# Gate and up products of both FFNs: six of eight couples of k-tiles as seven block products, one weight sum made by an accumulating transfer

## The reference

```python
def swiglu_ffn(x, w_gate_up, w_down):
    gate, up = jnp.split(x @ w_gate_up, 2, axis=-1)
    return (jax.nn.silu(gate) * up) @ w_down
...
        h = h + swiglu_ffn(rms_norm(h, ffn_norm_g[layer]), ffn_w_gate_up[layer], ffn_w_down[layer])
```

## Time and profile before

| | |
|---|---|
| median of 3 runs | 2800.21 us (2799.41 to 2800.48) |
| profiled execution, its own time | 2803.94 us |
| its span, first to last instruction | 2802.1 us |
| PE busy | 2739.6 us, 98% |
| DVE busy | 2219.6 us, 79% |
| ACT busy | 1648.4 us, 59% |
| POOL busy | 31.0 us, 1% |
| TensorE clock granted | 0.995 of 2.4 GHz |
| HBM read | 489.86 MB |

### The profile page before, as it was taken

The page is one execution under the profiler, slowest core; times in us unless marked ns, Lnnn a source line. Parts: engine busy times, 40 slices in busy tenths (PEclk is TensorE's granted clock), DMA queues, the critical chain, the costliest instruction groups (busy, mean ns, idle before and its releaser), DMA issues.

```text
span 2802.1 us, 40252 instructions
## 1 busy us (share of the span) xinstructions
PE 2739.6 (98%) x13456; PEld 2282.1 (81%) x13456; DVE 2219.6 (79%) x2727; ACT 1648.4 (59%) x2184; POOL 31.0 (1%) x30
## 2 busy tenths in 40 slices
PE   8999999999988999999999999999999999999998
PEld 6878888888877888888888888888887888888887
DVE  5867877878767788888888876557677888888887
ACT  6766767667665555555555555554555555555554
POOL 0000000000000000000000000000000000000000
PEclk9999999999999999999999999999999999999999
DMA  6534444445433566656666656643345666656664
GB/s 239 181 124 153 159 144 163 156 149 167 158 105 113 166 210 199 198 185 203 198 198 203 198 172 224 222 135 114 106 158 188 207 199 200 199 184 200 198 201 166
DMA packets 135097, 493.23 MB, mean 176 GB/s; under 512 B 15009, under 2 KB 15329, under 8 KB 134625
## 3 DMA queue, kind: packets, MB, share of 16 engines
q1 hardware_dynamic: 133776, 487.82, 52.8%
q10 hardware_dynamic: 1232, 4.23, 0.4%
HBM read 489.86 MB, written 2.13 MB: 176 GB/s over the span
## 4 chain that ended last, share of the span: by engine, by line
PE 65%; issue 29%; DVE 3%; ACT 2%; DMA 1%; POOL 0%; POOLq 0%; DVEq 0%; SPq 0%; ACTq 0%
PE ACC L733 10%; PE ACC L735 10%; PE ACC L734 10%; PE SIDE L943 7%; PE SIDE L944 7%; PE SIDE L945 7%; PE ACC L943 3%; PE ACC L944 3%; PE ACC L945 3%; PE SIDE L741 2%; DVE W_LO L1627 1%; DMA RAW<-stream 1%; PE SIDE L1138 1%; ACT W_HI L1194 0%; ACT WORK L1587 0%
## 5 line engine op out<-in xcount | busy, mean ns | idle before, releaser
L1627 DVE TENSOR_TENSOR W_LO<-RAW,W_HI 128x1024 fp32r<-128x1024 f32 x424 | 511.6, 1222 | 268.9 <-ACT W_HI L1194 265.8
L1194 ACT ACTIVATE W_HI<-RAW 128x1024 fp32r<-128x1024 f32 x424 | 443.3, 1057 | 217.5 <-PE ACC L735 183.8
L1436 ACT ACTIVATE W_HI<-WORK 128x1024 fp32r<-128x1024 f32 x320 | 325.4, 1031 | 345.8 <-PE SIDE L945 232.7
L733 PE MATMUL ACC<-W_HI,X_HI 128*128 128x512 f32 x1216 | 491.2, 404 | 17.7 <-DVE W_LO L1627 17.6
L735 PE MATMUL ACC<-W_HI,X_LO 128*128 128x512 f32 x1216 | 477.6, 393 | 0.0
L734 PE MATMUL ACC<-W_LO,X_HI 128*128 128x512 f32 x1216 | 476.7, 392 | 0.0
L1878 DVE TENSOR_TENSOR W_LO<-WORK,W_HI 128x1024 fp32r<-128x1024 f32 x300 | 364.5, 1221 | 119.0 <-ACT W_HI L1436 116.3
L1436 ACT ACTIVATE W_HI<-RAW 128x1024 fp32r<-128x1024 f32 x328 | 314.8, 980 | 237.0 <-PE ACC L735 141.6
L733 PE MATMUL ACC<-W_HI,A_HI 128*128 128x512 f32 x928 | 370.3, 399 | 0.7 <-issue 0.7
L735 PE MATMUL ACC<-W_HI,A_LO 128*128 128x512 f32 x928 | 362.7, 391 | 0.0
L734 PE MATMUL ACC<-W_LO,A_HI 128*128 128x512 f32 x928 | 362.2, 390 | 0.0
(11 more groups left out here) (363 smaller groups left out, 3798.7 us busy)
## 6 DMA issues: line engine op xcount, KB each, us to landing
RAW<-stream SPq DMA_DIRECT2D x752, 512.0 KB, 4.6
WORK<-stream SPq DMA_DIRECT2D x160, 512.0 KB, 4.8
WORK<-gdn_rows ACTq DMA_DIRECT2D x8, 512.0 KB, 6.2
WORK<-xt SPq DMA_DIRECT2D x4, 512.0 KB, 9.3
H<-x SPq DMA_DIRECT2D x2, 1024.0 KB, 13.6
out<-WORK SPq DMA_DIRECT2D x4, 512.0 KB, 3.5
WORK<-tails SPq DMA_DIRECT2D x2, 512.0 KB, 10.8
WORK<-gfin SPq DMA_DIRECT2D x1, 1024.0 KB, 6.6
```

The lines of the kernel that those rows point to most:

```text
L733: nc.tensor.matmul(dst, hi[:, at:at + P], wh, start=first and h % 2 == 0 and q == 0, stop=False)
L1194: nc.scalar.activation(W_HI[:, h % WS, :], raw_piece(h), ACT.Copy).then_inc(hi_ready, 1)
L1436: nc.scalar.activation(dst, src, ACT.Copy).then_inc(hi_ready, 1)
L1627: nc.vector.tensor_tensor(W_LO[:, h % WS, :], raw_piece(h), W_HI[:, h % WS, :].bitcast(f32), SUB).then_inc(lo_ready, 1)
```

## The change

Six couples of a block are made by seven products and two plainly, in the order "s pa s pb s s pa s s pb" ("s" for the four operations of a seven). A block has 36 operations (UP = 28 of gate and up, then 8) and 270 matmuls. The wide sum t13 is no longer made on DVE: SyncE loads the pair of blocks a second time, straight into one of three t13 buffers (`next_base`), and GpSimd issues a transfer that reads B12 from DRAM, twice over, and adds it to that buffer (`sum_pool`). DVE waits for it in `ffn_lo` ahead of the first half of t24, ACT ahead of the copy of "13". The token sums are made for six couples. `hid_lo` moves from e = 20 to e = 14, `dif` from e = 22 of 24 to e = 27 of 28.

```diff
-FFN_PIECE = {"11": 0, "21": 1, "13": 0, "24": 0, "pa": 2, "pb": 3}
-FFN_ORDER = 4 * ["11 21 13 24 pa pb"]
...
+SEVENS, PLAINS = 6, 2
+FFN_ORDER = "s pa s pb s s pa s s pb".replace("s", "11 21 13 24").split()
...
+UP = len(FFN_ORDER)
+BLK = UP + 8
...
+IN_STREAM = [{"11": (j, 0), "21": (j, 1), "pa": (SEVENS + j, 0), "pb": (SEVENS + j, 1), "d": (8 + j // 2, j % 2)}[kind]
+             for kind, j, piece in FFN_OPS if piece is not None]
+READ_LAST = {"11": "21", "21": "13"}
+RAW_FREE = [FFN_AT[READ_LAST.get(kind, kind), j] for kind, j, piece in FFN_OPS if piece is not None]
+MORE = (BLK - 24) * (FBLK - 1)
 RING = 6
+RING_LESS = 8 * (FBLK - 1)
+BASES = 3
+BASE_FREE = [-6, -4, -2] + [FFN_AT["13", j - BASES] + 1 for j in range(BASES, SEVENS)]
...
+        t24, c_add, dif, c_sum = w(5120, 1024), w(8192, 2048), w(7168, 512), w(10240, 2048)
+        t13 = [w(4096, 1024), VN[:, :], w(6144, 1024)]
+        hid_t, z_sum, z_more, x_sum = w(12288, 1024), w(6144, 2048), w(11264, 1024), w(8192, SEVENS * 512)
...
-            kt = 4 * j + (2 if kind[0] == "p" else 0)
+            kt = 2 * j + (2 * SEVENS if kind[0] == "p" else 0)
...
+            f, l = j == 0, j == (PLAINS if kind[0] == "p" else SEVENS) - 1
...
-                act.wait_ge(t_done, sums_done(ph, it, wrap) + (3 * j + (1 if kind == "13" else 3)))
-                src = t13 if kind == "13" else t24
+            if kind == "13":
+                act.wait_ge(t13_sum[j % BASES], base_n(base, it, wrap, j))
+                src = t13[j % BASES]
+            elif kind == "24":
+                act.wait_ge(t_done, sums_done(ph, it, wrap) + (2 * j + 2))
+                src = t24
...
-                    act.wait_ge(w_used, c + 19)
+                    nc.scalar.activation(YB[:, :], z_more, ACT.Copy).then_inc(z_hi, 1)
+            for e in range(0 if first or final_ else UP):
+                if e == FFN_AT["11", SEVENS - 1] + 2:
+                    act.wait_ge(w_used, c + e - 1)
                     nc.scalar.activation(c_add[:, 0:COLS], ACC[0][:, 0:COLS], ACT.Copy).then_inc(m1_out, 1)
...
-            raw = raw_at(base, it, wrap, kind, piece)[0]
             if kind == "21":
+                raw = raw_at(base, it, wrap, kind, piece)[0]
                 nc.vector.tensor_tensor(lo[:, 0:COLS], raw[:, COLS:2 * COLS], hi[:, 0:COLS], SUB).then_inc(lo_ready, 1)
-            else:
-                src = {"13": t13, "24": t24}.get(kind, raw)
-                nc.vector.tensor_tensor(lo, src, hi, SUB).then_inc(lo_ready, 1)
-            for n in range(3):
-                weight_sum(dve, ph, base, ob, it, e + 2 - n, n)
-
-        def weight_sum(dve, ph, base, ob, it, e, n):
-
-            (kind, j, piece), wrap = ffn_ahead(it, e)
-            if kind != "11":
+                dve.wait_ge(t_done, sums_done(ph, it, wrap) + (2 * j + 1))
+                nc.vector.tensor_tensor(t24[:, COLS:2 * COLS], t24[:, 0:COLS], raw[:, COLS:2 * COLS], ADD)\
+                  .then_inc(t_done, 1)
                 return
-            b11_22, b12_21 = (raw_at(base, it, wrap, kind, p)[0] for p in (piece, piece + 1))
-            done = sums_done(ph, it, wrap) + 3 * j
-            if n < 2:
-                dve.wait_ge(lo_ready, ffn_c(ob, it) + (e - 3 + n))
-            if n == 0:
-                for p in (piece, piece + 1):
-                    dve.wait_ge(*raw_at(base, it, wrap, kind, p)[1:])
-                i = nc.vector.tensor_tensor(tiles2(t13), tiles2(b11_22),
-                                            b12_21[:, 0:COLS].unsqueeze(1).broadcast_to([P, 2, COLS]), ADD)
-            else:
-                dve.wait_ge(t_done, done + n)
-                a = (t13 if n == 1 else t24)[:, 0:COLS]
-                b = (b11_22 if n == 1 else b12_21)[:, COLS:2 * COLS]
-                i = nc.vector.tensor_tensor(t24[:, (n - 1) * COLS:n * COLS], a, b, ADD)
-            i.then_inc(t_done, 1)
+            src = t13[j % BASES] if kind == "13" else t24 if kind == "24" else raw_at(base, it, wrap, kind, piece)[0]
+            nc.vector.tensor_tensor(lo, src, hi, SUB).then_inc(lo_ready, 1)
+            if kind == "11":
+                dve.wait_ge(lo_ready, ffn_c(ob, it) + e)
+                dve.wait_ge(t13_sum[j % BASES], base_n(base, it, wrap, j))
+                nc.vector.tensor_tensor(t24[:, 0:COLS], t13[j % BASES][:, 0:COLS], src[:, COLS:2 * COLS], ADD)\
+                  .then_inc(t_done, 1)
 
...
+                    dve.wait_ge(side_out[r], norm.after(f"norm{2 - r}", 0))
+                hi, lo = (b[:, 0:SEVENS * 512].bitcast(f32) for b in (X_HI, X_LO))
+                nc.vector.tensor_tensor(x_sum, hi, lo, ADD).then_inc(z_step, 1)
             elif k == 3:
                 dve.wait_ge(z_step, n + 1)
-                nc.vector.tensor_tensor(z5, a21, a22, SUB).then_inc(z_step, 1)
-                nc.vector.tensor_tensor(z7, a11, a21, SUB)
+                for a11, a21, a12, a22, z5, z7, z6, z3 in parts:
+                    i = nc.vector.tensor_tensor(z5, a21, a22, SUB)
...
+            for e in range(0 if first or final_ else UP):
+                if e == FFN_AT["pa", PLAINS - 1] - WS:
                     hid_lo(it, A_HI, A_LO)
-                if e == 22:
-                    dve.wait_ge(w_used, c + 22)
+                if e == FFN_AT["24", SEVENS - 1] + 1:
+                    dve.wait_ge(w_used, c + e)
                     dve.wait_ge(m1_out, it + late)
                     nc.vector.tensor_tensor(dif, ACC[0][:, COLS:2 * COLS], c_add[:, 0:COLS], SUB).then_inc(acc_out[0], 1)
                 ffn_lo(dve, ph, base, ob, it, e + WS)
...
+        def sum_pool(pool, base, it):
+
+            for j in range(SEVENS):
+                pool.wait_ge(t13_in[j % BASES], base_n(base, it, 0, j))
+                b12 = stream[it * 12 + (base - 4 + j)][:, PIECE:PIECE + COLS]
+                nc.gpsimd.dma_start(tiles2(t13[j % BASES]), b12.unsqueeze(1).broadcast_to([P, 2, COLS]),
+                                    accum_op=ADD).then_inc(t13_sum[j % BASES], 16)
+
...
+                def next_base(it, j):
+                    sp.wait_ge(lo_ready, ffn_c(ob, it) + BASE_FREE[j])
+                    if j == 2 and isinstance(it, int):
+                        sp.wait_ge(z_lo, 4 if ob == O_FFN0 else 8)
+                    sp.dma_start(t13[j % BASES], stream[it * 12 + (base - 4 + j)][:, 0:PIECE]).then_inc(t13_in[j % BASES], 16)
...
```

More of the change, by code:

```diff
@@ L64, with ffn_ops @@
 CHUNKS = B_FFN1 + C_FFN
-FFN_PIECE = {"11": 0, "21": 1, "13": 0, "24": 0, "pa": 2, "pb": 3}
-FFN_ORDER = 4 * ["11 21 13 24 pa pb"]
-FFN_OPS = [(kind, j, 4 * j + FFN_PIECE[kind]) for j in range(4) for kind in FFN_ORDER[j].split()] +     [("d", n, 16 + n) for n in range(8)]
-FFN_AT = {op[:2]: e for e, op in enumerate(FFN_OPS)}
-RAW_FREE = [FFN_AT[kind, j] for j in range(4) for kind in ("11", "21", "pa", "pb")] + [24 + n for n in range(8)]
-MORE = 8 * (FBLK - 1)
+SEVENS, PLAINS = 6, 2
+FFN_ORDER = "s pa s pb s s pa s s pb".replace("s", "11 21 13 24").split()
+def ffn_ops():
+    ops, seen, pieces = [], {}, 0
+    for kind in FFN_ORDER + 8 * ["d"]:
+        j = seen.get(kind, 0)
+        seen[kind] = j + 1
+        loaded = kind not in ("13", "24")
+        ops.append((kind, j, pieces if loaded else None))
+        pieces += loaded
+    return ops
+FFN_OPS = ffn_ops()
+UP = len(FFN_ORDER)
+BLK = UP + 8
+FFN_AT = {op[:2]: e for e, op in enumerate(FFN_OPS)}
+IN_STREAM = [{"11": (j, 0), "21": (j, 1), "pa": (SEVENS + j, 0), "pb": (SEVENS + j, 1), "d": (8 + j // 2, j % 2)}[kind]
[3 more added lines that the diff above has]
+MORE = (BLK - 24) * (FBLK - 1)
 RING = 6
+RING_LESS = 8 * (FBLK - 1)
+BASES = 3
+BASE_FREE = [-6, -4, -2] + [FFN_AT["13", j - BASES] + 1 for j in range(BASES, SEVENS)]
 O_FFN0 = 2 * B_FFN0
@@ L999, in ffn_tensor @@
                     products(pe, c, 2 * k + half, k // 4, X_HI, X_LO, k % 4 == 0, k % 4 == 3, 4 * (k % 4))
-            for e in range(0 if first or final_ else 24):
+            for e in range(0 if first or final_ else UP):
                 if e == 0:
@@ L1022, in ffn_tensor @@
                 for half in range(2):
[L1023 removed]
+                    products(pe, c, UP + 2 * k + half, k % 2, *((B_HI, B_LO) if final_ else (A_HI, A_LO)), True, True)
                 if final_ and nxt and k:
@@ L2353, in _ @@
                 gdn_pool(pool, it)
-            for nth in range(1, 4):
-                rstd_pool(pool, chain.link, nth)
+            rstd_pool(pool, chain.link, 1)
+            with pool.Fori(1, FBLK) as it:
+                sum_pool(pool, B_FFN0, it)
+            rstd_pool(pool, chain.link, 2)
+            rstd_pool(pool, chain.link, 3)
+            with pool.Fori(1, FBLK) as it:
+                sum_pool(pool, B_FFN1, it)
             for t in range(NT):
```

113 lines of the change are left out of this document (65 added, 48 removed).

## The result

The changed kernel takes 2851.78 us (median of 4 runs, 2848.3 to 2853.93), the kernel before, on the same chip, 2799.81 us. The ratio is 1.0182, 95% interval 1.0168 to 1.0196: 52 us slower. The forecast was 2810, "slower", with a range up to 2880. The direction came out, but only a part of the time comes from where I had looked for it: 10 us were forecast, and the 52 lie in the range only because a rival had widened it to 2880.

A forecast was written before the change was run, and what follows sets the result against it. A block was taken as bound by PE's number of matmuls. -1.36 (removed) + 0.85 (`hid_lo`) + 1.00 (`dif`) = +0.49 us a block, +9.8 us over 20 blocks, gave 2810 us; range 2784 to 2880.

The forecast's parts named there:

- the two chains: DVE's work ahead of "pa" behind `hid_lo` and ahead of `dif`: PE loses 0.85 and 1.00 us a block.
- The removed matmuls: On PE, 276 to 270 matmuls a block: 1.36 us less, 27.2 us over 20 blocks.
- It just holds, and costs nothing: Wide sums by DMA: load and sum take 9.6 to 14.6 us, with some 15 us of room, so no cost.
- the bounds of the same rows: An accumulating transfer's time to landing: at least a plain one's 4.8 us, at most 15.3 us, the slowest of that size.
- only two places: PE waits for DVE at "pa" behind `hid_lo` and at `dif`, together 0.55 to 1.85 us a block; 1.85 taken.
- mine: The main case: DVE in arrears at `hid_lo` and `dif`, sums free; 2810 us, own range 2803 to 2817, chance 0.40.
- the first rival, sums late: DVE, then PE, wait for late wide sums: 3 us once a block adds 60 us, 2870; up to 2910; chance 0.32.
- DVE is not behind: DVE reaches both places with four pieces in hand; only 0.55 us a block lost, -16 us, 2784; chance 0.10.
- half of it: One of PE's two waits comes as worked out, the other shorter: 2795 to 2806 us; chance 0.18.
- still fits: DMA engines, an add counted as two transfers: 42 x 1.26 = 53 us of a block's 63.

The follow-up runs named there:

- e8: The changed kernel without its six accumulating transfers a block and with `dif` one step earlier, timing only: 2799.3 us, 1.0000 of the kernel before.
- e4: The changed kernel without accumulating transfers, `hid_lo` moved to e = 8 and `dif` one step earlier, timing only: 2783.8 us, 0.9936 of the kernel before.
- e1: The changed kernel without its six accumulating transfers a block, ACT and DVE waiting for the base load instead, timing only: 2819.3 us, 1.0063 of the kernel before.
- e3: The changed kernel with all sums kept, `hid_lo` moved to e = 8 and `dif` one step earlier: 2868.2 us, 1.0233 of the kernel before.
- e2: The changed kernel with GpSimd's transfers overwriting the buffer instead of adding, timing only: 2825.3 us, 1.0089 of the kernel before.
- e11: e4 with the six accumulating transfers a block put back, into two tiles that nobody reads, timing only: 2795.1 us, 0.9985 of the kernel before.

## Why the prediction was right, and where not

**Right: the two chains.** `dif` was priced at 1.00 us a block and PE's timeline shows 1.00; taking it away gave 18.5 of 20.0 us. `hid_lo` was priced at 0.85; PE's timeline shows 0.74, the blocks of e8 and e4 differ by 0.77, and taking it away gave 17.0 of 17.0 us, a match to the tenth that is luck. The removed matmuls gave their 27.2, as far as the distance of two, still 0.227, shows it; no run put them back alone.

**Failed: "It just holds, and costs nothing".** That was the term for the sums. It had three parts. Transfers at 1.26 us each, the rate of the loads at the kernel's start: they take 1.48 us here, and the earlier trace rows would have told it, 0.59 x 63.47 / 24 = 1.56. An accumulating transfer at a plain one's price on the engines: 3.01 us, so the share came out at 0.95, not 45 of 63. And its way from issue to landing at 7.3 us, "as it is nearest to a queue that is 70% full": 10.4 in the median, behind a load of 7 and an instruction of 1.20 us. I left out that instruction, and set 14.6 us against 15, with no reserve, where the bounds of the same rows went to 4.8 + 15.3 = 20.1. The measured 19 lies near that upper bound. The term is 33.7 us (e1 against the change), not 0.

**Failed: only two places.** e4 stands at -17.2 where 27.2 were removed, so 10.0 us were still missing. A third place, the split of "13" in the second couple of each pair, accounts for 0.4 us a block, 8 us, by PE's timeline; the other 2 are open. My own chain, ended one stop earlier, gives it. From the moment the first couple's "11" leaves its slot, DVE needs 1.29 + 1.135 + 3 x 0.60 + 1.22 + 0.05 = 5.50 us to the split of the second couple's "13", PE 24 matmuls, 5.44 us. I had put DVE's chain against PE at `hid_lo` and `dif` only, and not at the splits between.

The account in us: -27.2 removed, +10.0 third place and rest, +17.0 `hid_lo`, +18.5 `dif`, +33.7 sums, together +52.0. It closes because the terms are differences between runs, and it holds for this order of steps alone: with DVE's order mended first the sums cost 84.4 us (e3 against e4), not 33.7. Even without them the kernel is 18.3 us slower than before, so the direction did not hang on the term that failed.

**The rivals.** The case that came true is mine together with the first rival, sums late; its condition, load plus sum over 15 us, is met. The sums cost 1.1 us a block and 9 us at the starts of the two parts, where its price of 60 us assumed 3 us a block and nothing at the starts. I had given them 0.40 and 0.32 as if they excluded each other. "DVE is not behind" and "half of it" did not come true. On the skill's rule (the Trainium skill, Collectives: The Full Stack, section "The bandwidth ceiling: the fold count and why AG ≠ RS ≠ AR"), that an add reads two sources and so goes at half the rate: the trace agrees by the size, 3.01 us for an accumulating transfer against 1.48 for a plain load, a factor of 2.03; against the same instruction without the add (e2) it is only 1.6, and no run shows the second read itself. My conclusion from it, that it "still fits", was drawn with 1.26 us a transfer; 42 x 1.48 = 62 us of a block of 63 would have said that nothing is left to spare.

## What to carry to other kernels

Where a transfer takes over an engine's work, price it from a steady stretch of the same kernel and not from its start, and set the whole chain (load, the issuing instruction, the second transfer) against the room that its buffers give; if it only just fits, call it late. More buffers and less traffic are not two ways to the same gain: here each alone left the kernel 48 us or more behind the old one, and both together brought it ahead. And an edit that speeds up one engine can make the kernel slower while another limit stands: e3's order lost 15 us with the sums and won 35 without them. Where many short waits of PE remain, look at the granted clock of the blocks as well.

## What was not expected of the hardware

- The same instruction without the add (e2: half rows of 2 KB, read twice) took 0.082 x 2823.4 / 120 = 1.93 us of all engines, with the add 0.130 x 2848.8 / 120 = 3.09, and a plain load of whole rows 1.48. With the add it went in 272 packets, without it in 144 (32640 and 17280 for 120 transfers); how much of the difference is the add itself and how much the smaller packets, no run tells.
- PE ran 500.00 of 500 us with the DMA engines at 0.99 and 302 GB/s (e11), so traffic near the limit did not by itself slow PE, ACT or DVE, whose instructions kept their lengths (DVE's split 1221 ns, ACT's copy 1057 ns, 1222 and 1057 before).
- GpSimd is busy for 1.20 us with each accumulating transfer and for 0.72 us with the plain one of e2. These are links of the chain from load to sum.
- After two waits of PE of about 1 us within 3 us the granted clock was at 0.58 and 0.56 in the next two windows of 2 us (e3, from 1306 us); before the first of them, which began at 1302.58, it had run for some 11 us without a gap, at a clock of 1.00.
